# A fused two-block transformer kernel: evacuations of PSUM one half later, background steps further apart, products of a tile pair reordered

## The chip, the cores and the metric

The kernel runs on one core of a Trainium2 chip. The metric is the device time of one execution in microseconds (us); lower is better. A core has TensorE (PE: matmuls, and the loads of their stationary operand, which the trace lists apart as PEld), VectorE (DVE), ScalarE (ACT), GpSimd (POOL) and SyncE (SP, which only starts transfers here). Each engine works through its own list of instructions in order, and the lists meet in semaphores.

## The reference, cut to what matters

One sequence of 256 tokens of width 2048 goes through two blocks, all in float32. Cut down:

```python
h = rmsnorm(x, mix_norm); proj = h @ w_in                       # 2048 x 7184
x = x + concat(stick_breaking_attention(sq, sk, sv), gated_deltanet(gq, gk, gv, gz, gb, ga)) @ w_out
x = x + memory_cross_attention(rmsnorm(x), rmsnorm(mem), w_xq, w_xkv, w_xo)
x = x + conv_ffn(rmsnorm(x), w_up, ffn_conv, ffn_conv_bias, w_down)   # 2048 -> 2 x 5632 -> 2048
x = rmsnorm(x, final_norm)
x = x + (fox_attention(q, k, v, log_f) * silu(gate)) @ fox_w_out      # after rmsnorm and fox_w_in
x = x + (swa_attention(rope(q), rope(k), v, sinks) * silu(gate)) @ swa_w_out
return rmsnorm(x, final_g_2)
```

Nearly all multiplications are products of 256 rows of activations with a weight matrix; every weight is read once.

## The kernel before, in words

**Two numbers for one.** Every float32 operand is split into a high part that TensorE multiplies at its fast float32 rate and a low part that holds the rest. A weight tile pair is split by ScalarE (`hi`: WH is a rounded copy of RAW) and VectorE (`lo`: WL = RAW - WH). The activations lie in A, B, H or M as [tile, high or low, token]. The product is high x high + high x low + low x high.

**Halves.** The weights come from `ws` in 512 KB loads (SyncE, into the ring RAW). Half of a load is 512 weight columns in 128 partitions, and is the unit of time of the whole program: `HALVES` lists 1416 of them, and `interleave` runs `main(j)` for half j on each engine and then one step of every background generator that is alive. `yield` or `ticks(n)` in a generator means: go on one half or n halves later. `T_...` constants say at which half a generator starts; `END[key]` and `ENDS[key, part]` are the last half of a weight chunk or of one of its two parts. WH and WL are rings of six halves; ScalarE works five halves ahead and VectorE four.

**Chunks.** `chunk_plan` gives the order: the eight input projections of the first block (`gq0`, `gk0`, `gv0`, `ba`, `gq1` ... `sv1`, `gz0`, `gz1`), `wo`, the memory attention (`xk`, `xq`, `xv`, `xo`), the FFN (`fg`, `fu`, `dn0`, `dn1`), the Fox layer (`fq`, `fk`, `ff`, `fv`, `ft`, `fo`) and the sliding-window layer (`wkv`, `wq`, `wt`, `w2`).

**Forms.** In the form "wide" (1256 of the 1416 halves) the weight tile is stationary. Per tile of the input and per 128 output features (t = 0, 1) one matmul multiplies WH by 512 columns, the 256 tokens' high parts and their low parts side by side, and one multiplies WL by the 256 high columns. Both add up in `P[:, t, :]`, a PSUM bank for each t. So a half is four pairs of a 512-column and a 256-column matmul, in the order 512 (t=0), 256 (t=0), 512 (t=1), 256 (t=1). "tokens" (the v projections) has the activations stationary and only 512-column matmuls; "plain" (`gq0`, `xo`) and "small" have only 256-column matmuls. Two PSUM slots of two banks take turns between parts (`slots[c % 2]`).

**Leaving PSUM.** After the last half of a wide part ScalarE copies the low columns out (`low`), VectorE adds the high columns to that copy (`evac`), and GpSimd multiplies by the norm factor RB (its `main`). All three do it in `main(j)` of that last half j; VectorE does so after `lo(j + 4)`. For `wo`, `dn`, `fo` and `w2` VectorE alone adds both parts to the residual XT.

**Background.** The gated delta rule (`octet`: Gram matrices and a blockwise triangular inverse for four heads; `recur`: the recurrence over chunks), stick-breaking attention (`sb`), the memory heads (`x_head`), the double norm after the FFN (`dnorm`), Fox and window attention (`fox`, `swa`) and the rotary embedding (`rope`) run in the banks ps4 to ps7 between the halves. Their steps on PE, DVE, ACT and POOL are written by hand with `ticks` between them, and each step waits on semaphores for its inputs. A wait in a background step stops PE's main stream, since PE has one list.

In `octet` ScalarE writes the decay factors exp(...) of two 128x512 tiles to t5; GpSimd multiplies GQ by t5; then VectorE reuses t5 for the values times beta, for which it waits for GpSimd (`w.wait_ge(qd_po, po + 4)`, L1084).

Of the kernel before, what the change touches and what calls it, by code (L numbers as in the profile page):

```python
# [166 lines left out]
def ticks(n):  # L167
    for _ in range(n):
        yield
# [33 lines left out]
NH = len(HALVES)  # L203
NS = NH // 2


T_XPREP = 0
T_NORM = {0: 7, 1: END["wo3"] + 4, 2: END["xo3"] + 6, 4: END["fo3"] + 4}
T_CONV = {(x, g): END[f"g{x}{g}"] + 1 for g in range(2) for x in "qkv"}
T_BA = END["ba"] + 1  # L210
T_L2 = {("q", 0): 24, ("k", 0): 40, ("q", 1): 76, ("k", 1): 92}
# [12 lines left out]
T_DN = [[ENDS[f"dn1_{n}", p] + 1 for p in range(2)] for n in range(4)]  # L224
T_DNORM = END["dn1_3"] + 6
T_XUP = END["dn1_3"] + 20
# [3 lines left out]
T_FO = [[ENDS[f"fo{n}", p] + 1 for p in range(2)] for n in range(4)]  # L230
# [4 lines left out]
T_W2 = [[ENDS[f"w2{n}", p] + 1 for p in range(2)] for n in range(4)]  # L235
# [6 lines left out]
def program(nc, xT, memT, ws, par, cst, cscr, out):  # L242
    with ExitStack() as ctx:
# [69 lines left out]
        t5, t6 = at("gt5", 53, [2, 4, 128])[:], at("gt6", 74, [2, 4, 128])[:]  # L313
        NT0, NT1 = at("NT0", 142, [512]), at("NT1", 144, [512])
# [132 lines left out]
        def tensor_program(e):  # L447
# [33 lines left out]
            def main(j):  # L481
# [91 lines left out]
            def octet(g):  # L573
# [23 lines left out]
                yield  # L597
# [6 lines left out]
                yield from ticks(2)  # L604
# [236 lines left out]
        def vector_program(e):  # L841
# [1194 lines left out]
```

## Time and profile before

| | |
|---|---|
| time, 3 runs | 2308.41 us median (2307.50 to 2313.97) |
| the profiled execution | 2308.81 us, of it span 2307.1 us |
| PE busy | 2243.9 us, 97% |
| DVE, ACT, POOL busy | 1637.0, 1299.6, 351.0 us (71%, 56%, 15%) |
| granted TensorE clock, mean | 0.992 |
| chain that ended last | PE 85%, DVE 8%, ACT 3%, POOL 2%, issue 2% |
| DMA | 387.5 MB, mean 168 GB/s |

Busy shares are averages over the span. A matmul's printed duration includes its way through the array and overlaps the next one; the distance between the starts of two neighbours is what a matmul costs. The waits view adds up, for each engine, the idle time ahead of an instruction and names the engine and tile whose semaphore ended it. The lines L451, L454 (PE), L851, L854, L857 (DVE), L1391 (ACT) and L1812 (POOL) are those of helpers; the tile names tell the steps apart: gt, GQ, GK, GV and VN belong to `octet` and `recur`, SBA and SBB to `sb`, XQ and memV to the memory heads, ACC to the norms, AQ and PTw to rope and `swa`.

### The profile page before, as it was taken

To read this page: it belongs to the slowest core of one execution; us is meant where nothing else is said; L and a number is where in the kernel's file an instruction comes from. 1 tells how busy PE (TensorE), PEld (TensorE's weight loads), DVE (VectorE), ACT (ScalarE), POOL (GpSimd) and SP (SyncE) were. 2 spreads that over 40 slices of the span, in tenths; PEclk is the share of its full clock that TensorE was granted. 3 is DMA by queue.
4 is the path that set the end of the run, shared out by engine and by line. 5 is a ranking of instruction groups with operands and counts; after the bars stand their busy time and mean duration, and the time that the engine had idled before them with its cause. 6 is when DMAs were issued, how large, how long until landed. Compare 5 with 4: busy or idle time off the path is not lost.

```text
span 2307.1 us, 35284 instructions
## 1 busy us (share of the span) xinstructions
PE 2243.9 (97%) x13792; PEld 1915.4 (83%) x13792; DVE 1637.0 (71%) x2722; ACT 1299.6 (56%) x2507; POOL 351.0 (15%) x295
## 2 busy tenths in 40 slices
PE   7989999999999999999999999999999999999998
PEld 7867888888888888888888888888888888877786
DVE  7767655568777778755777867766676777677776
ACT  6745335666565665544566655455556655555664
POOL 1121201113211111000111101211110101232202
PEclk9999999999999999999999999999999999999999
DMA  6432233464445555555555555555544555433353
GB/s 235 166 109 101 92 119 120 155 246 175 172 154 176 187 187 188 188 191 183 183 183 188 187 192 183 174 183 183 177 162 171 176 186 189 156 119 128 137 197 124
DMA packets 106326, 387.53 MB, mean 168 GB/s; under 512 B 11808, under 2 KB 12064, under 8 KB 105520
## 3 DMA queue, kind: packets, MB, share of 16 engines
q1 hardware_dynamic: 104400, 376.85, 46.8%
q0 software_dynamic: 1760, 8.42, 1.0%
q8 instruction: 109, 1.79, 0.3%
q14 instruction: 57, 0.47, 0.1%
HBM read 383.10 MB, written 2.13 MB: 167 GB/s over the span
## 4 chain that ended last, share of the span: by engine, by line
PE 85%; DVE 8%; ACT 3%; POOL 2%; issue 2%; DMA 0%; SPq 0%; DVEq 0%; POOLq 0%; ACTq 0%
PE main L451 77%; PE ps L451 7%; DVE WL L851 2%; DVE A L857 1%; PE ps L454 1%; ACT PPw L1391 1%; ACT WH L1391 1%; POOL AQ L1812 0%; DVE PPw L851 0%; DVE M L857 0%; DVE gt L851 0%; DVE XT L851 0%; POOL PPw L1962 0%; POOL ACC L1812 0%; DMA RAW<-ws 0%
## 5 line engine op out<-in xcount | busy, mean ns | idle before, releaser
L451 PE MATMUL main<-A,WH 128*128 128x512 f32 (+1 forms) x3680 | 1300.3, 399 | 15.6 <-DVE WL L851 13.3
L851 DVE TENSOR_TENSOR WL<-RAW,WH 128x512 fp32r<-128x512 f32 x1416 | 1064.7, 773 | 282.1 <-ACT WH L1391 277.9
L1391 ACT ACTIVATE WH<-RAW 128x512 fp32r<-128x512 f32 x1416 | 871.1, 626 | 579.2 <-PE main L451 575.9
L451 PE MATMUL main<-A,WL 128*128 128x256 f32 x3584 | 1009.9, 282 | 0.0
L451 PEld LDWEIGHTS main<-A,WH 128*128 128x128 f32 x3680 | 691.2, 190 | 189.7 <-DVE WL L851 16.9
L451 PEld LDWEIGHTS main<-A,WL 128*128 128x128 f32 x3584 | 682.4, 190 | 2.5 <-issue 1.9
L451 PE MATMUL main<-B,WH 128*128 128x512 f32 (+1 forms) x896 | 294.1, 381 | 2.6 <-DVE WL L851 2.6
L451 PE MATMUL main<-H,WH 128*128 128x512 f32 x704 | 248.8, 399 | 0.0
L451 PE MATMUL main<-B,WL 128*128 128x256 f32 x832 | 233.7, 281 | 0.0
L451 PE MATMUL main<-H,WL 128*128 128x256 f32 x704 | 197.9, 281 | 0.0
L451 PEld LDWEIGHTS main<-B,WH 128*128 128x128 f32 x896 | 164.1, 188 | 37.7 <-DVE WL L851 3.6
L451 PEld LDWEIGHTS main<-H,WH 128*128 128x128 f32 x704 | 132.3, 188 | 32.9
L451 PEld LDWEIGHTS main<-B,WL 128*128 128x128 f32 x832 | 157.6, 189 | 0.1
L1812 POOL TENSOR_TENSOR UB<-UB,RB 128x512 f32<-128x512 f32 x44 | 63.4, 1441 | 564.6 <-DVE UB L851 555.9
L451 PE MATMUL main<-WH,A 128*128 128x512 f32 (+1 forms) x448 | 138.2, 382 | 0.0
L451 PEld LDWEIGHTS main<-H,WL 128*128 128x128 f32 x704 | 133.1, 189 | 0.0
L1812 POOL TENSOR_TENSOR ACC<-ACC,SQ 128x1024 f32<-128x1024 f32 x20 | 52.3, 2613 | 368.9 <-ACT SQ L1391 368.9
L851 DVE TENSOR_TENSOR XT<-XT,main 128x512 f32<-128x512 f32 x88 | 60.1, 687 | 59.5 <-PE main L451 58.2
L451 PEld LDWEIGHTS main<-WH,A 128*128 128x128 f32 x448 | 82.3, 188 | 17.3 <-DVE WL L851 1.2
L1391 ACT ACTIVATE CC<-UB,PAR 128x256 f32<-128x256 f32 x88 | 52.2, 594 | 76.9 <-POOL UB L1812 76.9
L857 DVE SCALAR_TENSOR_TENSOR CC<-UB,PAR,CC 128x256 f32<-128x256 f32 x176 | 84.8, 482 | 5.8
L851 DVE TENSOR_TENSOR UB<-main,UB 128x512 f32<-128x512 f32 x44 | 30.4, 692 | 78.7 <-ACT UB L1391 78.7
(295 smaller groups left out, 1880.0 us busy)
## 6 DMA issues: line engine op xcount, KB each, us to landing
RAW<-ws SPq DMA_DIRECT2D x708, 512.0 KB, 3.3
CB<-cscr POOLq DMA_DIRECT2D x4, 1024.0 KB, 6.9
xs<-xT SPq DMA_DIRECT2D x8, 256.0 KB, 7.6
XT<-xT POOLq DMA_DIRECT2D x4, 512.0 KB, 7.4
MS<-memT POOLq DMA_DIRECT2D x4, 512.0 KB, 13.0
CST<-cst SPq DMA_DIRECT2D x1, 1056.0 KB, 7.7
out<-XT SPq DMA_DIRECT2D x2, 512.0 KB, 2.6
out<-XT SPq DMA_DIRECT2D x2, 256.0 KB, 2.1
```

Source lines behind the costliest of these rows:

```text
L451: return e.matmul(o, l, r, start=start, stop=True, skip_group_check=True)
L454: return e.transpose(o, i, ident)
L851: return e.tensor_tensor(o, a, b, op)
L857: return e.scalar_tensor_tensor(o, a, s, b, op0, op1)
L1391: return e.activation(o, i, f, bias=bias, scale=scale, accum_out=accum)
L1812: return e.tensor_tensor(o, a, b, op)
```

## The change

1. **Leaving PSUM.** VectorE and GpSimd no longer decide in `main(j)` whether half j ends a part; they go through a table `LEAVING[j]`. Wide and tokens parts and `gq0` stand there one half later than they end (exceptions: `xv` and `w23`); `xo`, `ba` and `ff` stand where they stood. VectorE thus does `lo` of the next half before it waits for the part's last matmul. ScalarE's `low` is not moved.
2. **Background.** Consumers start 1 to 3 halves later, and the steps within `octet`, `recur`, `sb` and `dnorm` lie further apart, mostly one half more per step; an octet takes about 44 halves where it took 36. `T_GOUT` and the second octet and recurrence move back accordingly.
3. **t7.** The decay factors get a buffer of their own, t7, and VectorE's wait for GpSimd before it writes t5 is gone.
4. **Order of products.** In a wide tile pair both 512-column matmuls come first, then both 256-column ones: 512 (t=0), 512 (t=1), 256 (t=0), 256 (t=1).

The instructions, their number, sizes and transfers are otherwise the same.

```diff
@@ tables @@
+LEAVING = [[] for _ in range(NH)]
+for _x, _e in ENDS.items():
+    LEAVING[_e if form_of(*_x) in ("plain", "small") and _x[0] != "gq0" or _x[0] in ("w23", "xv") else _e + 1].append(_x)
-T_CONV = {(x, g): END[f"g{x}{g}"] + 1 for g in range(2) for x in "qkv"}
+T_CONV = {(x, g): END[f"g{x}{g}"] + 4 for g in range(2) for x in "qkv"}
-T_OCTET = [62, 104]
-T_RECUR = [105, 143]
-T_GOUT = [126, 164]
+T_OCTET = [65, 110]
+T_RECUR = [110, 155]
+T_GOUT = [135, 180]
-T_GZ = [ENDS[f"gz{n // 2}", n % 2] + 1 for n in range(4)]
+T_GZ = [ENDS[f"gz{n // 2}", n % 2] + 3 for n in range(4)]
-T_WO = [[ENDS[f"wo{n}", p] + 1 for p in range(2)] for n in range(4)]
-T_HEAD = [ENDS["xq", n // 2] + 2 + 3 * (n % 2) for n in range(4)]
+T_WO = [[ENDS[f"wo{n}", p] + 2 for p in range(2)] for n in range(4)]
+T_HEAD = [ENDS["xq", n // 2] + 4 + 3 * (n % 2) for n in range(4)]
...
-T_FFN = {(u, j, p): ENDS[f"f{'gu'[u]}{j}", p] + 1 for j in range(11) for u in range(2) for p in range(2)}
+T_FFN = {(u, j, p): ENDS[f"f{'gu'[u]}{j}", p] + 3 for j in range(11) for u in range(2) for p in range(2)}
-T_DNORM = END["dn1_3"] + 6
-T_XUP = END["dn1_3"] + 20
+T_DNORM = END["dn1_3"] + 7
+T_XUP = END["dn1_3"] + 30
-T_QROPE = [[ENDS[f"wq{g}", p] + 2 for p in range(2)] for g in range(4)]
-T_SWA = [[END["wq0"] + 12 + 5 * (4 * g + p) for p in range(4)] for g in range(4)]
+T_QROPE = [[ENDS[f"wq{g}", p] + 4 for p in range(2)] for g in range(4)]
+T_SWA = [[END["wq0"] + 13 + 5 * (4 * g + p) for p in range(4)] for g in range(4)]
...
@@ tensor_program, main @@
+                        cols = [slice(256 * r + 128 * t, 256 * r + 128 * t + 128) for t in range(2)]
                         for t in range(2):
-                            cols = slice(256 * r + 128 * t, 256 * r + 128 * t + 128)
-                            mm(P[:, t, :], h[:, cols], both, start=first and r == 0)
-                            ins = mm(P[:, t, 0:T], l[:, cols], hi, start=False)
+                            mm(P[:, t, :], h[:, cols[t]], both, start=first and r == 0)
+                        for t in range(2):
+                            ins = mm(P[:, t, 0:T], l[:, cols[t]], hi, start=False)
@@ tensor_program, dnorm @@
-                yield from ticks(4)
+                yield from ticks(9)
                 w.wait_ge(s_fold, 4)
@@ vector_program, octet @@
-                w.wait_ge(qd_po, po + 4)
                 for b, o in enumerate((X, Z)):
                     w.wait_ge(qd_pe, pe + 4 + b)
                     tt(t5[:, b], four(o[:]), bc(beta[:, b, h4], 128), ALU.mult).then_inc(qd_ve, 1)
@@ vector_program, main @@
                 lo(j + LO_AHEAD)
-                key, part, i, n = HALVES[j]
-                if i == n - 1:
+                for key, part in LEAVING[j]:
                     evac(key, part)
@@ scalar_program, octet @@
-                    act(t5[:, b], four(o[:]), ACTF.Exp).then_inc(qd_ac, 1)
+                    act(t7[:, b], four(o[:]), ACTF.Exp).then_inc(qd_ac, 1)
@@ pool_program, main @@
-                key, part, i, n = HALVES[j]
-                if i < n - 1 or (key, part) not in SCALED:
-                    return
-                w.wait_ge(s_evac, CHUNK[key, part] + 1)
...
+                for key, part in LEAVING[j]:
+                    if (key, part) not in SCALED:
+                        continue
+                    w.wait_ge(s_evac, CHUNK[key, part] + 1)
...
```

## Rows read from the trace of the kernel before

**Rows 1.** Page, part 1: busy us (share of the span) and instructions
```profile
PE 2243.9 (97%) x13792; PEld 1915.4 (83%) x13792; DVE 1637.0 (71%) x2722; ACT 1299.6 (56%) x2507; POOL 351.0 (15%) x295
```

**Rows 2.** Groups by shape, PE: count, busy us, mean ns, idle before them
```profile
L451 PE MATMUL main<-A,WH 128*128 128x512 f32 x3488 | 1260.8, 404 | 2.6 <-DVE A L857 2.3 <-DVE WL L851 0.4
...
L451 PE MATMUL main<-B,WH 128*128 128x512 f32 x768 | 270.8, 397 | 2.6 <-DVE WL L851 2.6
L451 PE MATMUL main<-H,WH 128*128 128x512 f32 x704 | 248.8, 399 | 0.0
```

**Rows 3.** Stretches, PE on the main tiles: busy (count), clock, DMA share, GB/s
```profile
700.00:1400.00 700.00, 699.92 (x3961) 1.00 0.54 187
```

**Rows 4.** Timeline, PE, in w2: start us, us, instruction; pairs of 512 and 256
```profile
2219.94 0.39 PE L451 MATMUL main<-B,WH 128*128 128x512 f32 x1
...
2221.67 0.39 PE L451 MATMUL main<-B,WH 128*128 128x512 f32 x1
```

**Rows 5.** Timeline, PE, in fv1: 512-column matmuls only, three per row pair
```profile
1583.00 0.62 PE L451 MATMUL main<-WH,A 128*128 128x512 f32 x2
...
1586.40 0.62 PE L451 MATMUL main<-WH,A 128*128 128x512 f32 x2
```

**Rows 6.** Timeline, PE, in xo: 256-column matmuls only, three per row pair
```profile
673.90 0.40 PE L451 MATMUL main<-B,WH 128*128 128x256 f32 x2
...
676.78 0.40 PE L451 MATMUL main<-B,WH 128*128 128x256 f32 x2
```

**Rows 7.** Timeline, PE, in fg0, around two small transposes of a norm
```profile
704.25 0.39 PE L451 MATMUL main<-A,WH 128*128 128x512 f32 x1
...
705.64 0.39 PE L451 MATMUL main<-A,WH 128*128 128x512 f32 x1
...
705.98 0.38 PE L454 MATMUL ps<-CST,RB 128*128 128x128 f32 x2
...
706.56 0.40 PE L451 MATMUL main<-A,WH 128*128 128x512 f32 x1
...
707.62 0.40 PE L451 MATMUL main<-A,WH 128*128 128x512 f32 x1
```

**Rows 8.** Waits of PE, 100 to 300 us: us in total, times, longest us
```profile
PE ps L454 <- DVE gt L851: 5.0, 2, 4.8
PE ps L451 <- DVE gt L851: 4.6, 2, 2.9
PE ps L451 <- DVE gt L1090: 2.9, 1, 2.9
```

**Rows 9.** Waits over the whole span, of PE and at an evacuation of DVE
```profile
DVE UB L851 <- ACT UB L1391: 78.7, 43, 2.2
...
PE main L451 <- DVE WL L851: 16.0, 7, 8.4
PE main L451 <- POOL AQ L1812: 5.2, 7, 1.9
...
PE ps L451 <- POOL SBA L1890: 3.3, 3, 1.7
...
PE ps L451 <- ACT PTw L1391: 2.7, 3, 1.4
PE ps L451 <- POOL ACC L1812: 2.7, 2, 2.1
```

**Rows 10.** Timeline, DVE and POOL in octet 0, ahead of PE's longest wait
```profile
126.88 0.69 DVE L851 TENSOR_TENSOR PB<-main,PB 128x512 f32<-128x512 f32 x1 [4.16 <-ACT PB L1391]
...
129.28 3.00 POOL L1812 TENSOR_TENSOR GQ<-GQ,gt 128x512 f32<-128x512 f32 x2
...
134.07 2.53 DVE L857 SCALAR_TENSOR_TENSOR GQ<-PB,PAR,GQ 128x256 f32<-128x256 f32 x3
```

**Rows 11.** Timeline, PE, just after that wait
```profile
140.26 0.63 PE L451 MATMUL main<-A,WH 128*128 128x512 f32 x1
...
140.90 0.63 PE L451 MATMUL main<-A,WH 128*128 128x512 f32 x1
```

More of the change, by code:

```diff
@@ L313, in program @@
         t5, t6 = at("gt5", 53, [2, 4, 128])[:], at("gt6", 74, [2, 4, 128])[:]
+        t7 = at("gt7", 128, [2, 4, 128])[:]
         NT0, NT1 = at("NT0", 142, [512]), at("NT1", 144, [512])
@@ L595, in turned @@
                     z.then_inc(qd_pe, 1)
-                yield
+                yield from ticks(2)
                 w.wait_ge(l2_ve, 4 * g + 4)
@@ L603, in octet @@
                 mm(Z[:], K["ones"], fl(t6[:, 1])).then_inc(qd_pe, 1)
-                yield from ticks(2)
+                yield from ticks(3)
                 w.wait_ge(qd_ve, ve + 3)
@@ L622, in octet @@
                 cells(X, t3, K["eye"])
-                yield from ticks(2)
+                yield from ticks(3)
                 for lev in range(1, 6):
@@ L634, in octet @@
                     cells(Z, t3, t0)
-                    yield from ticks(2)
+                    yield from ticks(3)
                 w.wait_ge(qd_ve, ve + 26)
@@ L665, in recur @@
                         mm(O[:, 64 * n:64 * n + 64], ST[:, h, :], GQ[:, h, cs], start=n == 0)
-                    yield from ticks(2)
+                    yield from ticks(3)
                     w.wait_ge(rc_ve[g], c + 1)
@@ L690, in sb @@
                     mm(b[:, 256:384], K["negtri"], B[:, 256:384], start=False).then_inc(sb_pe[lane], 1)
-                    yield from ticks(3)
+                    yield from ticks(4)
                     w.wait_ge(sb_ac[lane], S_AC * i + 2)
@@ L1052, in octet @@
                     tt(t6[:, b], bm(K["triB"], 4), bc(gg[:, b, h4], 128), ALU.mult).then_inc(qd_ve, 1)
-                yield from ticks(2)
+                yield from ticks(3)
                 w.wait_ge(qd_pe, pe + 1)
@@ L1062, in octet @@
                 ts(t2, t0, 0.0, ALU.min).then_inc(qd_ve, 1)
-                yield from ticks(3)
+                yield from ticks(4)
                 w.wait_ge(qd_po, po + 1)
@@ L1091, in octet @@
                 for lev in range(1, 6):
-                    yield from ticks(2)
+                    yield from ticks(3)
                     if lev > 1:
@@ L1098, in octet @@
                     tt(t4, t4, eight(Z[:]), ALU.subtract).then_inc(qd_ve, 1)
-                yield from ticks(2)
+                yield from ticks(3)
                 for b, o in enumerate((X, Z)):
@@ L1111, in recur @@
                     tt(VN[P, 4 * g:4 * g + 4, :], four(X[P, :]), GV[P, 4 * g:4 * g + 4, ds], ALU.add).then_inc(rc_ve[g], 1)
-                    yield from ticks(2)
+                    yield from ticks(3)
                     w.wait_ge(rc_pe[g], 3 * c + 2)
@@ L1138, in sb @@
                     stt(B[:, 0:384], b[:, 0:384], 0.0, A[:, 0:384], ALU.max, ALU.add).then_inc(sb_ve[lane], 1)
-                    yield from ticks(6)
+                    yield from ticks(7)
                     w.wait_ge(s_Bh, kt + 1)
@@ L1218, in dnorm @@
             def dnorm():
-                yield from ticks(6)
+                yield from ticks(11)
                 w.wait_ge(dn_ac, 1)
@@ L1505, in octet @@
                 pe, ve = Q_PE * g, Q_VE * g
-                yield from ticks(2)
+                yield from ticks(3)
                 w.wait_ge(qd_pe, pe + 1)
@@ L1509, in octet @@
                 for b, o in enumerate((X, Z)):
-                    act(t5[:, b], four(o[:]), ACTF.Exp).then_inc(qd_ac, 1)
-                yield from ticks(2)
+                    act(t7[:, b], four(o[:]), ACTF.Exp).then_inc(qd_ac, 1)
+                yield from ticks(3)
                 w.wait_ge(qd_ve, ve + 5)
@@ L1529, in recur @@
                     cs = slice(64 * c, 64 * c + 64)
-                    yield from ticks(3)
+                    yield from ticks(4)
                     w.wait_ge(rc_pe[g], 3 * c + 3)
@@ L1564, in sb @@
                     act(A, b[:, 0:384], ACTF.Exp).then_inc(sb_ac[lane], 1)
-                    yield from ticks(3)
+                    yield from ticks(4)
                     w.wait_ge(sb_pe[lane], S_PE * i + 3)
@@ L1647, in dnorm @@
             def dnorm():
-                yield from ticks(5)
+                yield from ticks(10)
                 w.wait_ge(dn_pe, 1)
@@ L1855, in octet @@
                 pe, ve, ac = Q_PE * g, Q_VE * g, Q_AC * g
-                yield from ticks(4)
+                yield from ticks(6)
                 w.wait_ge(qd_ac, ac + 3)
@@ L1870, in octet @@
                 for lev in range(1, 5):
-                    yield from ticks(4)
+                    yield from ticks(5)
                     w.wait_ge(qd_pe, pe + (9 if lev == 1 else 5 + 3 * lev))
@@ L1890, in sb @@
                     e.affine_select(out=diag(A[:]), in_=diag(A[:]), **keep).then_inc(sb_po[lane], 1)
-                    yield from ticks(5)
+                    yield from ticks(6)
             def reload():
```

30 lines of the change are left out of this document (15 added, 15 removed).

## Prediction, made before the changed kernel was run

> **What bounds the kernel now.** I read the page's busy line first: PE is busy for 97% of the span, no other engine for more than 71% [rows 1]. So time can only come from two places: from the 63 us in which PE does nothing (2307.1 less 2243.9), and from how closely the matmuls follow each other while it is "busy". An engine other than PE matters only where PE waits for it.
>
> For the second place I looked at starts, not durations. The wide form has 3488 + 768 + 704 = 4960 pairs of a 512- and a 256-column matmul [rows 2], besides 64 of the memory keys, 5024 in all. From 700 to 1400 us PE does nothing else: 3961 matmuls in 700 us, 353.4 ns a pair, at full granted clock [rows 3]. At 2220 us the same pair in the same order takes less: five pairs in 1.73 us, 346 ns [rows 4]. Streams of one size run as closely: 512-column matmuls fifteen in 3.40 us, 226.7 ns each [rows 5], 256-column ones twenty-four in 2.88 us, 120.0 ns each [rows 6]. 226.7 + 120.0 = 346.7 ns is just the faster of the two pair times. So the wide stream mostly runs in a rhythm that costs 6.7 ns a pair more than its matmuls do among their own kind. The timeline also shows how it falls into it: four pairs ahead of two small transposes take 1.39 us, 347.5 ns each, and three pairs after them 1.06 us, 353.3 ns each [rows 7]. A disturbance starts it, and the alternation of sizes keeps it up.
>
> For the first place I read PE's waits. They are for steps of the octets (5.0, 4.6 and 2.9 us) [rows 8], and over the whole span for WL (16.0: 2.6 in wo and 0.4 in a wide A stage [rows 2], so 13.0 in the first halves, where nothing is loaded yet), for AQ of rope (5.2), SBA (3.3), ACC (2.7) and PTw (2.7) [rows 9].
>
> **The change part by part.**
>
> *Order of products.* Nothing is added or removed; in a group of four matmuls the changes of size fall from four to two. There are 2512 groups. In the old order a group costs 706.8 ns in the slow rhythm and 693.4 in the fast one. I put the slow rhythm at four fifths of the pairs (an estimate: it fills rows 3, while w2, the first 100 us and patches after long stalls are fast), so 0.8 x 5024 x 6.7 ns = 27 us lie in it. No row of before shows the new order. If the loss comes with each change of size, half of it goes: 13 us. If the pair of 512s lets the stream settle as it settles in a stream of one size, all of it goes: 27 us. If the rhythm doesn't care about the order, nothing. I take 13, because the streams of one size show no loss at all and the new order stands halfway between them and the old one. The bounds are 0 and 27; below nothing is a rival of its own, under Rivals.
>
> The Trainium skill speaks against this part: "TensorE: Matmul & The Clock Gate", section "Back-to-back issue gap", makes the distance depend on the matmul's own columns alone (N / 2.4 + 2.5 ns), so any order of the same four costs the same. The same pair taking 346 and 353.4 ns, the longer one at full granted clock, disagrees with that [rows 3, 4]; the sum by the rule would have a 0 here.
>
> *Leaving PSUM a half later.* At an evacuation of the FFN VectorE has been sitting for 78.7 us in 43 cases, 1.8 us each, for ScalarE's `low`, which itself waits for PE's last matmul [rows 9]. A half lasts four pairs, 1.41 us. `lo` of the next half (0.69 us, as the evacuation itself takes [rows 10]) now goes into that wait instead of behind it. The evacuation hardly moves in time; WL of the next half comes earlier. That costs nothing, as the wait hides it. Behind the evacuation on DVE stand the next `lo` and the background steps, and in its place GpSimd's scaling stays right behind it. The slot is needed again a whole part (8 halves, 11 us) later, so PE doesn't feel it.
>
> *t7 and the octets.* PE's longest background wait, 4.8 us, is for VectorE's t6 and GK steps [rows 8]. Ahead of it DVE sat 4.16 us for an evacuation, then GpSimd's product with t5 took 3.00 us, for which t5 made VectorE wait, and three convolution steps took 2.53 us, 0.84 each for 256 columns, where the evacuation of 512 took 0.69 [rows 10]. t7 takes out the wait, the later evacuation moves `lo` ahead, the convolution starts 3 halves later, and each step has one half more. The three rows add up to 12.5 us, of single waits up to 4.8 us; one half is 1.41 us, so spacing alone does not clear them all. I take three quarters: 9.5 us. About 2.5 us of smaller waits in both octets and the recurrence I put at 1.5.
>
> The Trainium skill, "SBUF — State Buffer", section "SBUF: two separate sides", says that a GpSimd instruction and a VectorE one with two SBUF inputs lock each other out. The stretched convolution beside GpSimd's work would fit [rows 10]. By that rule t7 frees the order but not the port, and a part of this wait stays; that is one reason for three quarters.
>
> *sb, dnorm, rope, heads, wo.* SBA (3.3 us in 3, longest 1.7) gets one half more: 2.5 us saved. ACC (2.7, longest 2.1) gets six halves more: 2.7. AQ (5.2 us in 7, longest 1.9): rope comes two halves later, 2.8 us, while its input moves by at most one `lo`, 0.7 us: 5.2. The heads get two halves, 0.4. The 2.6 us for WL in wo [rows 2] come where VectorE also splits the memory, which isn't moved: 1.3. PTw is left as it is, as are the first halves' 13.0 and the 2.3 for A [rows 2].
>
> *Clock.* After the 4.8 us wait a pair starts 0.64 us after the last one, not 0.35, for about four pairs: the 1.2 GHz level instead of the 2.4 [rows 11]. 1.2 us for that one; with other stalls of some 3 us and the restarts, I count 3 us for all that go.
>
> *New costs.* Steps that feed main now end later: the last H tile ahead of dn1, gz ahead of wo, the gates ahead of fo and w2. Each had one or two halves to spare and loses up to one or two: 0 to 1.4 us each in five places, I take 1 us in sum, since a late tile stops only the last matmuls of its half. sb of group 1 starts in the half after sv1, now also the half of its evacuation; the wait that `lo` fills covers that. The second octet starts just when the first ends; a missed step there would cost one half. These stay in the range.
>
> *Sum.* 9.5 + 1.5 + 2.5 + 2.7 + 5.2 + 0.4 + 1.3 + 3 - 1 = 25 us for the schedule, and 13 for the order: 38 us. The profiled execution took 2308.8 us (span 2307.1), 0.4 above the median of the runs. 2308.8 - 38 = 2271; against the median 2270. I forecast 2270 us.
>
> **The rivals.**
>
> 1. *The order is worth nothing* (the rule quoted above, or a rhythm that is set by the small steps between the halves). For it: transposes start the slow rhythm whatever the order. Against it: streams of one size don't have it. 2308.4 - 25 = 2283 us. By the rule of "TensorE: Matmul & The Clock Gate" the time would come out here.
> 2. *The order is worth all of it.* Every group takes 693.4 ns: 2308.4 - 25 - 27 = 2256 us.
> 3. *The waits only move.* A chain's next step is late instead; the work of DVE and POOL in the octets is the same, and they share it with convolutions that now run elsewhere. Then only rope, dnorm, the heads and half of sb are saved, 10 us, and 13 for the order: 2285 us.
> 4. *Slower.* A 256 is the shortest cover that a stationary load has; with two in a row the stream, once disturbed, falls behind at each of them and at each 512 too, so that every matmul of a group pays the 6.7 ns that now every second one pays. A group would take 693.4 + 4 x 6.7 = 720 ns, 13.4 more than now; in 2512 groups 34 us, plus 5 where w2 and other fast stretches are lost, less 25: 2322 us. This comes out slower than before from a group of about 717 ns on. For it: nothing in the rows, as the order was never run. Against it: both uniform streams.
> 5. *Nothing changes*: order without effect and waits that move, with new costs for what rope saves. 2305 us.
>
> **How the numbers follow.** Forecast 0.38; rivals 1 to 5: 0.19, 0.17, 0.14, 0.06, 0.06. The range 2252 to 2292 holds the forecast and rivals 1 to 3 with some of their own spread, and leaves out both slow ones and the tails, somewhat under 2 in 10. A measurement of this kernel can tell about 0.3%, 7 us, from no change: faster than 2301.5 are the forecast and rivals 1 to 3 (0.88) and a little of 5, in all 0.88; within 7 us 0.06; slower 0.06.
>
> **What the profile after would show.** Order: PE in 700 to 1400 us would count about 3998 matmuls at 700 ns a group, 4037 at 693.4, 3961 if it does nothing, fewer than 3900 under rival 4. The PE waits for gt, AQ, ACC and SBA should be small or gone, those for PTw, memV and the start as they were; the evacuation rows of DVE should show less idle time ahead of them, with a WL in its place; the clock between 120 and 260 us should be nearer full. The prediction is wrong if the octets' waits come back under other names (rival 3), if new waits for WL appear, or if the wide stream runs slower at full clock.

## The result and the profile after

The changed kernel took 2254.17 us (median of 4 runs, 2253.88 to 2254.47), beside 2308.6 us before (4 runs, 2307.5 to 2313.97): a ratio of 0.9775 (95% interval 0.9755 to 0.9796), 54 us less. The forecast was 2270 with a range of 2252 to 2292; the time lies in the range, 2 us above its lower bound and next to the second rival (2256).

The page after, head and part 1 (as [rows 1]):

```profile
span 2252.7 us, 35286 instructions
PE 2216.2 (98%) x13792; PEld 1907.6 (85%) x13792; DVE 1644.7 (73%) x2722; ACT 1315.0 (58%) x2507; POOL 346.8 (15%) x295
```

PE's idle time fell from 2307.1 - 2243.9 = 63.2 us to 2252.7 - 2216.2 = 36.5: 26.7 of the 54 us. The rest has to be in what counts as busy. The stretch of [rows 3] after:

```profile
700.00:1400.00 700.00, 700.00 (x4021) 1.00 0.55 189
```

4021 matmuls stood in for 3961: 696.3 ns a group of four, for 706.8. PE's waits over the whole span (us in total, times, longest), as [rows 8, 9]:

```profile
PE main L456 <- DVE WL L857: 15.0, 6, 7.7
PE ps L459 <- DVE gt L857: 3.1, 2, 2.8
PE main L456 <- DVE A L863: 2.4, 2, 1.5
PE ps L456 <- DVE memV L860: 1.5, 1, 1.5
PE ps L456 <- ACT PTw L1395: 1.3, 2, 1.0
PE ps L456 <- ACT SQ L1395: 1.3, 1, 1.3
PE main L456 <- DVE AQ L857: 0.7, 1, 0.7
PE main L456 <- POOL AQ L1816: 0.4, 1, 0.4
PE ps L456 <- ACT gt L1395: 0.2, 1, 0.2
PE ps L456 <- DVE GV L1107: 0.2, 1, 0.2
```

SBA and ACC are gone, gt and AQ are small, and no new name is over 0.7 us. These rows add up to 26.1 us; those of before to 53.0. VectorE's waits (same columns) show the later evacuation:

```profile
DVE WL L857 <- ACT WH L1395: 389.3, 532, 3.6
DVE UB L857 <- ACT UB L1395: 27.7, 43, 0.7
...
DVE XT L857 <- PE main L456: 11.2, 5, 6.9
```

UB's 78.7 us [rows 9] are 27.7 now, and the idle time stands ahead of `lo` instead (WL 389.3, before 277.9), where it harms nobody. The residual's wait for PE's last matmul (XT) went from 58.2 to 11.2.

Last the clock, in stretches where it was low. Columns: stretch, then busy us and count of PE, PEld, DVE, ACT and POOL, granted clock, DMA share, GB/s. Before, then after:

```profile
120.00:140.00 20.00, 14.73 (x134) 12.56 (x133) 15.23 (x23) 8.32 (x16) 8.87 (x6) 0.89 0.24 81
140.00:160.00 20.00, 17.08 (x155) 14.04 (x154) 12.50 (x22) 10.29 (x17) 2.53 (x2) 0.85 0.34 125
180.00:200.00 20.00, 17.09 (x219) 14.95 (x218) 12.82 (x21) 10.15 (x18) 2.81 (x2) 0.91 0.31 107
240.00:260.00 20.00, 19.15 (x145) 16.69 (x144) 16.45 (x27) 4.97 (x9) 5.88 (x5) 0.91 0.23 80
```

```profile
120.00:140.00 20.00, 16.69 (x147) 14.25 (x146) 17.71 (x27) 10.77 (x19) 8.99 (x6) 0.99 0.24 85
140.00:160.00 20.00, 20.00 (x182) 17.09 (x181) 16.71 (x27) 12.56 (x21) 4.23 (x3) 0.92 0.44 155
180.00:200.00 20.00, 20.00 (x237) 16.70 (x236) 11.89 (x20) 12.90 (x24) 2.56 (x2) 1.00 0.40 134
240.00:260.00 20.00, 20.00 (x180) 17.61 (x178) 13.87 (x26) 5.67 (x10) 2.27 (x2) 1.00 0.38 133
```

Each percent under full clock in 20 us is 0.2 us of matmul time, or less where PE waits anyway: (11 + 15 + 9 + 9) x 0.2 = 8.8 us before, (1 + 8) x 0.2 = 1.8 after. The change took most of the waits out of these stretches, and with them went most of the 1.2 GHz level. Two more stretches are at 0.91 in both kernels: 20 to 40 us, and just behind `xo` (680 to 700 us before, 660 to 680 after).

### The profile page after: what moved, and what is told of

It is laid out like the page before. It is cut to its first block, busy times and chain, and to the rows that moved or that the text cites. A ratio compares the mean times of both kernels' runs of the same rounds, so it can differ in the third digit from the quotient of the medians.

```text
span 2252.7 us, 35286 instructions
## 1 busy us (share of the span) xinstructions
PE 2216.2 (98%) x13792; PEld 1907.6 (85%) x13792; DVE 1644.7 (73%) x2722; ACT 1315.0 (58%) x2507; POOL 346.8 (15%) x295
## 4 chain that ended last, share of the span: by engine, by line
PE 91%; DVE 5%; ACT 2%; issue 1%; POOL 1%; DMA 0%; SPq 0%; DVEq 0%; POOLq 0%; ACTq 0%
PE main L456 83%; PE ps L456 7%; DVE WL L857 1%; PE ps L459 1%; DVE A L863 1%; DVE M L863 1%; ACT WH L1395 0%; DVE XT L857 0%; ACT PPw L1395 0%; DMA RAW<-ws 0%; POOL PPw L1966 0%; DVE gt L857 0%; DVE GQ L863 0%; DVE PPw L857 0%; ACT A L1395 0%
## 5 line engine op out<-in xcount | busy, mean ns | idle before, releaser
L857 DVE TENSOR_TENSOR WL<-RAW,WH 128x512 fp32r<-128x512 f32 x1416 | 1065.3, 765 | 399.5 <-ACT WH L1395 389.3
L456 PE MATMUL main<-A,WH 128*128 128x512 f32 (+1 forms) x3680 | 1156.9, 397 | 15.5 <-DVE WL L857 12.3
L456 PE MATMUL main<-A,WL 128*128 128x256 f32 x3584 | 716.3, 279 | 0.0
L456 PEld LDWEIGHTS main<-A,WH 128*128 128x128 f32 x3680 | 567.5, 190 | 38.5 <-DVE WL L857 17.1
L456 PE MATMUL main<-B,WH 128*128 128x512 f32 (+1 forms) x896 | 265.4, 380 | 2.7 <-DVE WL L857 2.7
L456 PE MATMUL main<-H,WH 128*128 128x512 f32 x704 | 221.1, 395 | 0.0
L456 PE MATMUL main<-B,WL 128*128 128x256 f32 x832 | 169.0, 278 | 0.0
L456 PEld LDWEIGHTS main<-B,WH 128*128 128x128 f32 x896 | 137.1, 189 | 3.5 <-DVE WL L857 3.3
L456 PE MATMUL main<-H,WL 128*128 128x256 f32 x704 | 138.3, 278 | 0.0
L456 PE MATMUL main<-WL,A 128*128 128x512 f32 (+1 forms) x224 | 84.1, 375 | 0.0
L857 DVE TENSOR_TENSOR XT<-XT,main 128x512 f32<-128x512 f32 x88 | 60.0, 686 | 12.6 <-PE main L456 11.2
L1395 ACT ACTIVATE PPw<-PPw,SM 128x128 f32<-128x128 f32 (+1 forms) x64 | 28.4, 444 | 49.3 <-DVE SM L860 49.3
```

The source lines that it names most:

```text
L456: return e.matmul(o, l, r, start=start, stop=True, skip_group_check=True)
L857: return e.tensor_tensor(o, a, b, op)
L1395: return e.activation(o, i, f, bias=bias, scale=scale, accum_out=accum)
```

## The experiments

### The two halves of the change

**order_only**: before with the new order of products alone; **order_undone**: after with the old order.

```diff
@@ order_only; order_undone is the reverse, in after @@
+                        cols = [slice(256 * r + 128 * t, 256 * r + 128 * t + 128) for t in range(2)]
-                            cols = slice(256 * r + 128 * t, 256 * r + 128 * t + 128)
-                            mm(P[:, t, :], h[:, cols], both, start=first and r == 0)
-                            ins = mm(P[:, t, 0:T], l[:, cols], hi, start=False)
+                            mm(P[:, t, :], h[:, cols[t]], both, start=first and r == 0)
+                        for t in range(2):
+                            ins = mm(P[:, t, 0:T], l[:, cols[t]], hi, start=False)
```

> The kernel before with the new order of products alone. Theory (each change of matmul size keeps the slow rhythm going): the wide stretch from 700 to 1400 us counts about 4020 matmuls instead of 3961, as in the changed kernel, and the time falls by about 18 us to 2290 us, while the waits for gt, AQ, ACC and SBA stay as before. Rival (the changed kernel's closer stream comes from fewer disturbances by background steps): 3961 matmuls there and 2308 us.

> The changed kernel with the old order of products. Theory: 3961 matmuls from 700 to 1400 us and about 2272 us, 18 above the changed kernel; the waits stay as short as in it. Rival (fewer disturbances): about 4020 matmuls and 2254 us.

Measured: order_only 2291.22 us (2290.63 to 2292.83), ratio 0.9932 (0.9916 to 0.9949); order_undone 2270.84 (2269.0 to 2271.84), ratio 0.9844 (0.9829 to 0.9859). Main tiles on PE, 700 to 1380 us, of before, order_only, order_undone and after:

```profile
700.00:1380.00 680.00, 679.92 (x3848) 1.00 0.54 186
```
```profile
700.00:1380.00 680.00, 679.92 (x3903) 1.00 0.59 189
```
```profile
700.00:1380.00 680.00, 680.00 (x3851) 1.00 0.58 186
```
```profile
700.00:1380.00 680.00, 680.00 (x3907) 1.00 0.55 189
```

In these four the rate of the stream follows the order, whatever the schedule, and PE's waits follow the schedule, whatever the order (in order_only gt 5.0, 4.6 and 2.9, SBA 3.4 and ACC 2.7 us, as before). So does the clock: between 120 and 260 us order_only still has four stretches at 0.80 to 0.94, and order_undone has none below 1.00. The two parts add: 0.9932 x 0.9844 = 0.9777, the measured ratio is 0.9775. The order is worth 2270.84 - 2254.17 = 16.7 us, the schedule 0.0156 x 2308 = 36 us.

### What of the order of products counts

Three readings were open: the sizes' alternation, the PSUM bank to which neighbours add, or only the length of a run of one size. **one_bank** keeps 512, 512, 256, 256 but does all four for one bank and then all four for the other. **crossed** keeps the old alternation of sizes and moves the change of bank: in the old order it lies between a 256 and the next 512, in crossed between a 512 and the 256 behind it. **four_512** makes runs of four of a size in each half, **mirror_512** runs of eight across two halves (odd halves begin with their 256s).

```diff
@@ one_bank @@
-                    for r in range(2):
...
+                    for t in range(2):
+                        for r in range(2):
+                            c0 = 256 * r + 128 * t
+                            mm(P[:, t, :], h[:, c0:c0 + 128], fl(Xs[r][:, 2 * i + r, :, :]), start=first and r == 0)
+                        for r in range(2):
+                            c0 = 256 * r + 128 * t
+                            ins = mm(P[:, t, 0:T], l[:, c0:c0 + 128], Xs[r][:, 2 * i + r, 0, :], start=False)
@@ crossed @@
+                        for t, long in ((0, True), (1, False), (1, True), (0, False)):
...
@@ four_512 @@
-                            mm(P[:, t, :], h[:, cols[t]], both, start=first and r == 0)
+                            mm(P[:, t, :], h[:, c0:c0 + 128], fl(X[:, 2 * i + r, :, :]), start=first and r == 0)
+                    for r in range(2):
...
@@ mirror_512 @@
+                    long = [(r, t, True) for r in range(2) for t in range(2)]
+                    short = [(r, t, False) for r in range(2) for t in range(2)]
+                    for r, t, wide in (long + short if i % 2 == 0 else short + long):
...
```

> The changed kernel with all four 512-column matmuls of a half first, then its four 256-column ones: two changes of size per half instead of four. In the kernel before a half took 1413 ns in the slow rhythm (eight changes), in the changed one 1393 (four); without loss it would be 1387. Theory (loss by changes of size): 1387 to 1390 ns a half, 4 to 8 us less, 2246 to 2250 us. Rival (what is left is a fixed loss per half, such as its semaphore wait): 1393 ns and 2254 us.

> As the version with four 512s first, but every second half runs its 256-column matmuls first, so that eight of a kind follow each other across halves: one change of size per half. Theory: the half takes 1387 ns, about 2246 us. Rival (fixed loss per half): 2254 us. If runs of one size let the stream fall behind instead, it is slower than the version with four.

> The changed kernel with the same order of sizes (512, 512, 256, 256), but both tiles of the half go to the first bank and then both to the second, where the changed kernel changes banks at every matmul. Theory (the order of sizes sets the rhythm): 1393 ns a half, 3907 matmuls from 700 to 1380 us, 2254 us. Rival (adding to the bank that the last matmul wrote is what costs): back to 1413 ns, about 3850 matmuls, 2271 us.

> The changed kernel with the old order of sizes (512, 256, 512, 256) and the banks crossed: 512 to the first, 256 to the second, 512 to the second, 256 to the first. Theory (sizes): about 3850 matmuls from 700 to 1380 us and 2271 us, as with the old order. Rival (banks): about 3907 and 2254 us.

Main tiles on PE, 700 to 1380 us, of one_bank, crossed, four_512 and mirror_512:

```profile
700.00:1380.00 680.00, 679.52 (x3902) 1.00 0.57 189
```
```profile
700.00:1380.00 680.00, 680.00 (x3851) 1.00 0.56 187
```
```profile
700.00:1380.00 680.00, 680.00 (x3877) 1.00 0.58 188
```
```profile
700.00:1380.00 680.00, 679.50 (x3892) 1.00 0.58 189
```

| kernel | runs of a size | time, us | ratio (95%) | half of 8, ns |
|---|---|---|---|---|
| order_undone | 1 | 2270.84 | 0.9844 (0.9829 to 0.9859) | 1413 |
| crossed | 1 | 2271.58 | 0.9851 (0.9822 to 0.9880) | 1413 |
| after | 2 | 2254.17 | 0.9775 (0.9755 to 0.9796) | 1392 |
| one_bank | 2 | 2257.10 | 0.9791 (0.9767 to 0.9814) | 1394 |
| four_512 | 4 | 2262.89 | 0.9810 (0.9795 to 0.9825) | 1403 |
| mirror_512 | 8 | 2260.10 | 0.9796 (0.9782 to 0.9811) | 1398 |

The last column is 8 x 680 us over the count. Banks fall out: one_bank has after's rate and crossed has the old one. (one_bank is 3 us longer elsewhere; it needs a half's second input tile earlier, and PE's waits for A and H are 1.5 us longer in sum. The rest of the 3 us stays open.) The sizes it is; but "fewer changes of size cost less", on which four_512 and mirror_512 were expected to gain, is wrong. With a half of 4 x 346.7 = 1387 ns as the floor, the excess per run of 512s is 6.5 ns for runs of one, about 3 for two, 16 for four and 22 for eight. Their timelines on PE (start us, us; a row is one run) say where it lies. four_512, then mirror_512:

```profile
1001.06 1.09 PE L456 MATMUL main<-H,WH 128*128 128x512 f32 x4
1001.99 0.63 PE L456 MATMUL main<-H,WL 128*128 128x256 f32 x4
1002.46 1.09 PE L456 MATMUL main<-H,WH 128*128 128x512 f32 x4
```
```profile
1000.64 1.11 PE L456 MATMUL main<-H,WL 128*128 128x256 f32 x8
1001.60 2.00 PE L456 MATMUL main<-H,WH 128*128 128x512 f32 x8
1003.44 1.12 PE L456 MATMUL main<-H,WL 128*128 128x256 f32 x8
```

The 256s keep their pace (eight in 1001.60 - 1000.64 = 0.96 us, 120 ns each). The 512s don't: four in 0.93 us, 232 ns each, eight in 1.84 us, 230 ns each, where a stream of them alone has 226.7 [rows 5]. So 512s that follow a run of 256s go slowly for several matmuls. The single starts in mirror_512's trace say for how many: averaged over the 242 runs of eight between 700 and 1380 us, the 512s take 233, 236, 228, 233 and 231 ns, and the last three 226.7 each. In after the 512s are no quicker (233 ns each), but the two 256s take 115 and 116 ns, less than the 120 of a stream of their own, and that is where the group gains. A run of two is the best of the four lengths tried. What in TensorE does that, the rows don't say.

### The old order has two rhythms, the new one has one

**leaving_only**: before with the table `LEAVING` and nothing else.

```diff
+LEAVING = [[] for _ in range(NH)]
+for _x, _e in ENDS.items():
...
@@ vector_program and pool_program, main @@
+                for key, part in LEAVING[j]:
...
```

> The kernel before with the later place for leaving PSUM alone (the LEAVING table for VectorE and GpSimd); starts, spacings, t5 and the order of products as before. Undoing it in the changed kernel cost 12 us, most of it in waits for PTw, which were only 2.7 us in the kernel before. Theory (it gives something wherever VectorE's list is the late one): the waits for gt and PTw shrink, 2297 us. Rival (it only makes room for the wider spacing and by itself leaves steps that follow it at once too early): 2305 us or more, with longer waits of PE for AQ.

Measured: 2289.73 us median, but of the four runs two took 2282.45 and 2282.85 and two 2296.61 and 2299.78; ratio 0.9935 (0.9889 to 0.9981). The profiled run is one of the shorter. PE's stretch, and five pairs of its timeline:

```profile
700.00:1380.00 680.00, 680.00 (x3925) 1.00 0.56 191
```
```profile
1000.29 0.39 PE L455 MATMUL main<-H,WH 128*128 128x512 f32 x1
...
1002.02 0.39 PE L455 MATMUL main<-H,WH 128*128 128x512 f32 x1
```

Five pairs in 1.73 us, 346 ns, in the old order: this run kept the fast rhythm through the FFN, at 1386 ns a half faster even than the new order. The count there is 77 above the 3848 of before, 13 us of matmuls, and PE's waits fell from 53.0 us to 43.3: together 23 us, about what the two shorter runs gained over the 2306.67 us of the kernel before beside them; the waits alone give about what the two longer ones gained. So the gap of 14 to 17 us between runs of one program fits a stream that holds the fast rhythm in some executions and loses it in others; the slower two have no trace here, so that is inferred. The kernel before has single short runs as well: most are near 2307, one took 2296.46 and one 2291.33.

In before the slow rhythm began right behind the norm's two small transposes [rows 7]. leaving_only has the same two, and behind them the fast rhythm goes on:

```profile
688.07 0.38 PE L458 MATMUL ps<-CST,RB 128*128 128x128 f32 x2
...
689.33 0.39 PE L455 MATMUL main<-A,WH 128*128 128x512 f32 x1
...
692.80 0.39 PE L455 MATMUL main<-A,WH 128*128 128x512 f32 x1
```

Ten pairs in 3.47 us, 347 ns each. The same disturbance thus starts the slow rhythm in one execution and not in another. The slow rhythm itself isn't an even one: by the single starts in before's trace (from 800 us on) its pairs take 350, 350 and 360 ns in turn, 353 on average.

The four runs of after lie within 0.6 us, and those of each variant with the new order within 1.2 to 3.9 us. (order_undone and crossed, old order with the whole new schedule, were steady too, within 2.8 and 4.1 us, in the slow rhythm.) The new order doesn't reach the best rate, 696.3 ns a group against 693.4, but every traced run of it keeps this rate from 700 to 1380 us.

As for PE's waits in leaving_only, theory and rival both came true in part: gt fell to 3.2 + 1.5 + 1.1 us from 5.0 + 4.6 + 2.9 and PTw (2.7) is gone, while AQ rose from 5.2 to 9.6: here rope wasn't given the two halves more that the change gives it.

### Which part of the schedule earns the 36 us

**leaving_undone**: after with the evacuations where they stood. By the order of the lists the FFN's steps can't then come three halves later (the evacuation of the first `dn1` part would stand ahead of VectorE's step for an H tile that PE needs in the same half), so `T_FFN` went back to +1 with it; the wide spacing there depends on the later leaving. **t7_undone**: after with one buffer t5 and VectorE's wait. **octet_undone**: after with the times, the spacing and t5 of the octets and recurrences as before.

```diff
@@ leaving_undone @@
-    LEAVING[_e if form_of(*_x) in ("plain", "small") and _x[0] != "gq0" or _x[0] in ("w23", "xv") else _e + 1].append(_x)
+    LEAVING[_e].append(_x)
-T_FFN = {(u, j, p): ENDS[f"f{'gu'[u]}{j}", p] + 3 for j in range(11) for u in range(2) for p in range(2)}
+T_FFN = {(u, j, p): ENDS[f"f{'gu'[u]}{j}", p] + 1 for j in range(11) for u in range(2) for p in range(2)}
@@ t7_undone @@
+                w.wait_ge(qd_po, po + 4)
-                    act(t7[:, b], four(o[:]), ACTF.Exp).then_inc(qd_ac, 1)
+                    act(t5[:, b], four(o[:]), ACTF.Exp).then_inc(qd_ac, 1)
@@ octet_undone: t7_undone, and @@
-T_OCTET = [65, 110]
-T_RECUR = [110, 155]
+T_OCTET = [62, 104]
+T_RECUR = [105, 143]
-                yield from ticks(3)
+                yield from ticks(2)
...
```

> The changed kernel with VectorE and GpSimd leaving PSUM in the half in which a part ends, as before; the FFN's steps start at one half after it, as before; all other starts and spacings stay changed. Theory (the later place fills a wait of VectorE and gives PE nothing by itself): VectorE's idle time ahead of UB is back near 79 us, PE's waits stay as in the changed kernel, 2254 to 2258 us. Rival (the evacuation that blocks VectorE's list is what made PE wait in the octets): the waits for gt return, 2262 us or more.

> The changed kernel with the decay factors in t5 again and VectorE's wait for GpSimd's product back. Theory (t7 takes out part of the longest octet wait): the wait of PE for gt ahead of the transposes of GK grows from 2.8 by 1 to 3 us, 2255 to 2257 us. Rival (the spacing alone has made room for GpSimd): 2.8 us as in the changed kernel, 2254 us.

> The changed kernel with everything of the octets, the recurrence and the gated rule's starts as before (ticks, T_CONV, T_L2, T_OCTET, T_RECUR, T_GOUT, t5 with its wait). Theory (the spacing took 12 us of waits for gt and VN and some of the clock behind them): 2266 us, with PE waiting 12 us for gt. Rival (the later leaving alone cleared these waits): 2254 to 2257 us.

| kernel | time, us (runs) | ratio (95%) | against after |
|---|---|---|---|
| leaving_undone | 2266.33 (2264.48 to 2268.35) | 0.9831 (0.9807 to 0.9855) | +12.2 |
| t7_undone | 2254.32 (2252.15 to 2254.61) | 0.9777 (0.9753 to 0.9800) | 0 |
| octet_undone | 2256.73 (2255.98 to 2257.50) | 0.9789 (0.9756 to 0.9821) | +2.6 |

t7 is worth nothing, where 1 to 3 us were expected. Before's own timeline of VectorE shows why:

```profile
137.12 1.28 DVE L851 TENSOR_TENSOR gt<-ps,SM 128x512 f32<-128x512 f32 x2
```

This is the write to t5 that had to wait for GpSimd's product. The product had ended at 129.28 + 3.00 = 132.28 us [rows 10], 4.8 us earlier, and no idle time stands ahead of the write; in the second octet the two times are 242.95 and 247.13. The wait had always been met when VectorE came to it.

The later leaving, which was put at nothing for PE, costs 12 us to undo in the changed kernel. The octets' spacing, on which the forecast put the largest share, costs 2.6 once the later leaving is there, as octet_undone's rival had it. The two overlap: PE's waits for steps of the octets and the recurrence are 15.3 us before, 5.2 in leaving_undone (spacing without the later leaving), 6.6 in octet_undone (the reverse) and 3.5 in after. Either of the two clears most of them. (The intervals of the ratios, 0.9789 and 0.9775, are too wide to tell 2.6 us; it rests on the waits, which are 3.1 us apart.) In leaving_undone the rival named the time, but its reason failed: the waits for gt did not return. PE by stretch from 1900 us on (busy and count, clock), leaving_undone and then after:

```profile
1900.00:2220.00 320.00, 309.23 (x1892) 1.00 0.45 151
```
```profile
1900.00:2220.00 320.00, 317.60 (x1944) 1.00 0.44 156
```

The two profiled runs are 13.9 us apart, and 8.4 of these lie here, in the sliding-window layer. PE's waits in leaving_undone from 2000 us on:

```profile
PE ps L456 <- ACT PTw L1395: 4.9, 5, 2.3
PE ps L456 <- DVE PTw L1307: 2.3, 2, 1.3
```

PTw, in after 1.3 us, is 7.2 here. VectorE's list has an evacuation at the end of every wide part, which sits in its queue until PE's last matmul and ScalarE's copy are done, and every softmax step of VectorE behind it sits too. In the later place it waits little (UB 27.7 us in 43, 0.6 each), and the whole queue moves up. In the FFN the same wait (UB 74.7 us in leaving_undone) costs PE nothing: PE is busy for all 680 us from 700 to 1380.

The 12 us are a price within the changed schedule. In before, with the early leaving, PTw was only 2.7 us; something else in the new schedule makes the early leaving dearer there, and what it is was not tried. The 12.2, 0 and 2.6 us of the table leave more than half of the 36 without an experiment of their own: rope, `sb`, `dnorm` and the heads, whose waits fell by 10.5 us, were never undone alone, and the clock takes up part of the rest.

### What was left: GpSimd's sum beside VectorE's splits

PE's two waits for A in after (0.9 us ahead of 665.9 and 1.5 ahead of 668.4) come at the end of the memory attention's residual. GpSimd, then VectorE there:

```profile
663.01 2.48 POOL L1816 TENSOR_TENSOR ACC<-ACC,SQ 128x1024 f32<-128x1024 f32 x1 [3.65 <-ACT SQ L1395]
665.57 2.48 POOL L1816 TENSOR_TENSOR ACC<-ACC 128x512 f32<-128x512 f32 x2
```
```profile
662.16 0.48 DVE L863 SCALAR_TENSOR_TENSOR A<-XT,PAR,A 128x256 fp32r<-128x256 f32 x1
...
663.16 2.62 DVE L863 SCALAR_TENSOR_TENSOR A<-XT,PAR,A 128x256 fp32r<-128x256 f32 x1
```

The split takes 0.48 us alone and 2.62 beside GpSimd's sum, which starts 0.15 us earlier and takes 2.48. VectorE's instruction ends 0.3 us after GpSimd's, and `lo` behind it (665.70, 1.76 us) and the next split (667.39, 0.94 us) fall beside GpSimd's second sum. Two kernels tried to move them apart. **pool_later** gives GpSimd's sum a later place in its list (and starts three other background steps later); **squares_later** is that, and ScalarE's squares come three halves later too.

```diff
@@ pool_later @@
-            parts += [(T_WO[n][1] + 2, residual("wo", n)) for n in range(4)] + [(T_XO[n] + 3, residual("xo", n)) for n in range(4)]
+            parts += [(T_WO[n][1] + 2, residual("wo", n)) for n in range(4)] + [(T_XO[n] + (6 if n == 3 else 3), residual("xo", n)) for n in range(4)]
-T_MEM = END["gz1"] + 10
+T_MEM = END["gz1"] + 13
-T_NORM = {0: 7, 1: END["wo3"] + 5, 2: END["xo3"] + 6, 4: END["fo3"] + 5}
+T_NORM = {0: 7, 1: END["wo3"] + 5, 2: END["xo3"] + 8, 4: END["fo3"] + 5}
-T_FFN[0, 0, 0] = END["xo3"] + 14
+T_FFN[0, 0, 0] = END["xo3"] + 16
@@ squares_later: pool_later, and in scalar_program, residual @@
                 if part != 0:
+                    if stage == "xo" and n == 3:
+                        yield from ticks(3)
                     squares(stage, n, XT[:, 4 * n:4 * n + 4, :])
```

> The changed kernel with GpSimd's sums moved away from VectorE's urgent steps: the memory stage starts 3 halves later, and the last sum of squares after xo and the fold behind it come 3 and 2 halves later, as does the first FFN step. In the changed kernel VectorE's split of M took 2.65 us beside a GpSimd sum of 2.41 where it takes 0.47 alone, and PE waited 2.7 us for WL in wo and 2.4 us for A after xo. Theory (the two engines lock each other out, so that what counts is where GpSimd's sums lie): both waits shrink to 1 us or less in sum, 2249 to 2251 us. Rival (VectorE simply has too much to do there): both stay, 2254 us.

> pool_later again, and beyond it ScalarE's squares of the last quarter of the memory attention's residual stand three halves later in its list. GpSimd's sum of squares (2.48 us) starts as soon as the squares are there, at 663 us, and lies beside VectorE's two splits of that residual, which take 2.6 us instead of 0.5; PE then waits 2.4 us for A. Theory (the sum is tied to ScalarE's squares, and the two engines share a port): with the squares later the sum runs behind both splits, these take 0.5 us each, the wait for A falls from 2.4 to under 0.5 us, and the time to 2249.5 us (2248.5 to 2250.5), if the norm's transposes still find their sum. Rival (the splits are late for another cause, VectorE's own list): the wait for A stays at 2.4 us and the time at 2252 us. A third way: the norm factor now comes too late and PE waits for ACC or RB instead, 2252 to 2255 us.

Measured: pool_later 2251.99 us (2251.44 to 2252.65), ratio 0.9768 (0.9736 to 0.9800). Neither theory nor rival held whole. The wait for A stayed at 2.4 us. With the memory's splits (`T_MEM`) later, PE's waits for WL between 380 and 520 us, in wo, fell from 2.7 us in after to 0.6:

```profile
PE main L456 <- DVE WL L857: 2.7, 3, 1.8
```
```profile
PE main L456 <- DVE WL L857: 0.6, 1, 0.6
```

But 1.1 us of waits for WL came up between 520 and 540 us, so that all of PE's waits fell by only 1.0 of the 2.2 us. Most of the rest is the clock: from 660 to 680 us it was 0.91 in after and 1.00 in pool_later, 1.8 us, although the same 2.4 us of waits for A lie in both. So a wait of this length is followed by the low level in one run and not in another, and a gain through the clock is less sure than one in the waits.

Measured for squares_later: 2249.57 us (2249.13 to 2250.70), ratio 0.9746 (0.9729 to 0.9763). GpSimd and VectorE in squares_later:

```profile
666.89 2.41 POOL L1818 TENSOR_TENSOR ACC<-ACC,SQ 128x1024 f32<-128x1024 f32 x1 [8.70 <-ACT SQ L1395]
```
```profile
662.99 0.47 DVE L863 SCALAR_TENSOR_TENSOR A<-XT,PAR,A 128x256 fp32r<-128x256 f32 x1
```

The wait for A is gone and the time fell by its 2.4 us; what GpSimd's sum now lies beside is `lo` (from 667.36 us three of them take 5.33 us), where PE has no wait. GpSimd waits for nothing that marks the halves, so its place in the list doesn't set its time; the semaphore that it waits on does. In pool_later the sum started at 662.41 us, against 663.01 in after; only moving ScalarE's squares moved it. This is the fastest kernel of the study, 4.6 us below after; the ranges of their runs lie apart (2249.13 to 2250.70 against 2253.88 to 2254.47), though the intervals of the two ratios overlap a little.

## Why the prediction was right, and where it was off

**What bounds the kernel.** That time could come only from PE's 63 us of idleness and from the spacing of matmuls held: 26.7 us came out of the first. The third place was weighed too lightly: the clock. (1 - 0.992) x 2307.1 = 18.5 us and (1 - 0.996) x 2252.7 = 9.0 us make 9.5 us, each mean rounded to about 1.2 us; it is an upper bound, since some of the low clock falls on waits. From run to run the mean is 0.991 to 0.994 for the kernel before and 0.995 or 0.996 for after. The order's 17 with them gives 53 of the 54.4 us of the span. The forecast was 16 us too long, and all of it points one way: 4 in the order, 5 in the waits and 6.5 in the clock were left out. That the time still lies in the range is owed to the room that it had for all 27 us of the order, and so to luck.

**Order of products: right direction, wrong mechanism.** The forecast was 13 us between 0 and 27, and 16.7 were measured. "The loss comes with each change of size, half of it goes" gave 700.1 ns a group; it is 696.3. The estimate that four fifths of the groups were slow was somewhat high: 0.8 x 2512 x (706.8 - 696.3) = 21 us gained there, less 0.2 x 2512 x 2.9 = 1.5 lost where the old order had been fast, make 20; the 16.7 fit seven tenths. The step that failed is "if the loss comes with each change of size, half of it goes": four_512 and mirror_512 have fewer changes and are slower, so that 13 against 16.7 was near by luck. "A disturbance starts it" holds for the trace of before alone; in leaving_only the same transposes don't. Rival 1 is out: the same eight matmuls take 1392, 1398, 1403 or 1413 ns by their order at full granted clock. The prediction put the rule of the Trainium skill, "TensorE: Matmul & The Clock Gate", section "Back-to-back issue gap", behind that rival. The section gives its formula for an isolated matmul and says that in a stream with weight loads both instructions set the spacing, so it spoke less clearly for rival 1 than the prediction has it. Rival 2 came near the time, but for another reason: the order gave 17 and not 27, and the schedule gave the rest. Rival 4 is out.

**Leaving PSUM: the step that failed.** "That costs nothing... so PE doesn't feel it" put this part at 0, and undoing it costs 12 us, in the changed schedule and together with the FFN's starts. The text named the background steps behind the evacuation on VectorE, but priced only the evacuation's own slot. For the FFN, where the row was read (UB 78.7 us), the zero holds; in the window attention (PTw 7.2 us against 1.3) and in the octets of leaving_only (15.3 us to 6.5) it doesn't.

**t7 and the octets: right sum, one cause wrong.** The waits of octets and recurrence fell from 15.3 us to 3.5, 11.8 against a forecast of 9.5 + 1.5. But t7 gave nothing: the prediction counted GpSimd's 3.00 us [rows 10] as a wait of VectorE, and VectorE never stood for it. "Spacing alone does not clear them all" holds, with 5.2 us left, but it clears ten, and the later leaving alone, which the prediction counted here as a help, clears nine. "A part of this wait stays" came true with 3.1 us. The convolution still runs beside GpSimd (three steps in 3.35 us at 126.88, two products of GpSimd in 2.89 us at 127.06); whether that is what holds the 3.1 us was not tried. (VectorE's wait that t7 removes stands at L1078 of the kernel before, not L1084.)

**sb, dnorm, rope, heads, wo.** SBA 3.3 (forecast 2.5), ACC 2.7 (2.7), AQ 5.2 to 1.1, so 4.1 (5.2), heads 0.4 (0.4): the sizes are close; no experiment took these parts singly. wo: WL there is 2.7 us against 2.6, nothing gained of 1.3; pool_later, which does move the memory's splits, gained 2.1 there and lost 1.1 just behind. PTw, left as it was, fell by 1.4. Two small ones that no step named, ahead of NT's transposes (1.1) and "issue" (1.2), went as well. All waits together: 26.9 us saved against 22.1.

**Clock.** 3 us forecast, up to 9.5 measured; this term was mis-sized. I had counted one stretch behind one wait; of seven stretches of 20 us at 0.85 to 0.91 five rose, the fifth of them (1440 to 1460 us, 0.91) in the double norm:

```profile
1440.00:1460.00 20.00, 17.33 (x89) 0.91 0.39 134
```
```profile
1440.00:1460.00 20.00, 20.00 (x120) 1.00 0.47 162
```

Schedule: 36 us where 25 were forecast; of the difference 4.8 lie in the waits and up to 6.5 in the clock. New costs were put at 1 us and none shows.

## What to carry to other kernels

An instruction that waits for the pipeline's end (an evacuation) should stand in its engine's list where its input is already there: its own time costs nothing, but everything behind it waits with it, and the price is to be read at the urgent steps of other stages, not at its own. Two remedies for the same wait overlap, so undo each with the other in place and count the waits, not only the time. Before giving a wait in the code a price, find it in the trace: the one that t7 removed was never waited for. When waits go, read the clock of every stretch around them as well; here it gave back up to a third of the waits' time, though not the same in every run. Where matmuls of two sizes alternate, measure the order: two of a kind made the rate steady, and four or eight of a kind were slower than two.

## What the runs showed of the hardware that was not expected

- 512- and 256-column matmuls in alternation run at 346.7 or 353.4 ns a pair, the slow rhythm as 350, 350, 360. Two small transposes start it in one trace (before) and not in another (leaving_only). The same program took 2282 us twice and 2297 and 2300 once; that the rhythm makes this gap is inferred. In the order 512, 512, 256, 256 the group took 696 or 697 ns in every trace.
- 512s behind a run of four or eight 256s take 230 to 232 ns on average instead of 226.7; in runs of eight the sixth is the first at 226.7. The excess per run of 512s goes 6.5, 3, 16, 22 ns for lengths 1, 2, 4 and 8. Its cause stays open, and so does what starts the slow rhythm.
- The PSUM banks of neighbours don't matter to the rate: 1394 against 1392 ns (one_bank and after), and 1413 against 1413 (crossed and order_undone).
- A 256-column VectorE step of 0.47 us takes 2.62 beside a GpSimd sum of 2.48. The Trainium skill, "SBUF — State Buffer", section "SBUF: two separate sides", says that the two engines lock each other out of a shared port. squares_later agrees: with the sum moved, the step is back at 0.47 us.
